# A decoder step on one core: cached latent pages issued from ScalarE's queue, and the first cached sequence's keys and the folding weights loaded during the late prompt attention

## The reference, cut to what matters

```python
def one_seq(args):                       # one of the 8 sequences
    pages, qb, cb, rb = args             # 16 pages of 128 rows, in any order
    c_past = cache_kv_latent[pages].reshape(-1, KV_LORA)      # 2048 x 256
    r_past = cache_k_rope[pages].reshape(-1, QK_ROPE_DIM)     # 2048 x 32
    ...
    k = mla_keys(c_all, r_all, w_uk, g_k_nope, g_k_rope)      # keys, RMS-normalised per head
    p = attn_probs(qb[None], k, mask)
    o_lat = jnp.einsum('bhql,blc->bqhc', p, c_all)            # probabilities times latents
    return jnp.einsum('bqhc,chv->bqhv', o_lat, w_uv)[0]
```

## Time and profile before

| | |
|---|---|
| median of 3 runs | 3511.48 us (3498.91, 3511.48, 3511.61) |
| profiled execution | 3516.18 us, span 3514.4 us |
| TensorE, VectorE, ScalarE, GpSimd busy | 2845.7, 2707.2, 968.1, 1765.9 us |
| DMA | 899.61 MB, mean 256 GB/s over the span |
| sample attention | about 863 to 1265 us of the span |
| late prompt attention | about 615 to 857 us |

### The profile page before, as it was taken

How to read it: one execution, slowest core, us unless ns; L and a number is a source line. 1 busy time by engine, 2 the same in 40 slices (tenths; PEclk the granted TensorE clock), 3 DMA queues, 4 the chain that set the end, 5 groups by cost and what they waited for, 6 DMA issues and landing times. The chain is left out here.

```text
span 3514.4 us, 40173 instructions
## 1 busy us (share of the span) xinstructions
PE 2845.7 (81%) x12509; PEld 2094.9 (60%) x12509; DVE 2707.2 (77%) x5283; ACT 968.1 (28%) x1627; POOL 1765.9 (50%) x1379
## 2 busy tenths in 40 slices
PE   6655697886888866656629799999999999999997
PEld 3444354665333333355618677787778777777775
DVE  3237687896878847759979688888888888888886
ACT  2212132432323311111108622222222222222221
POOL 0026455475545526626546445566666555555553
PEclk9677798876989977787859899999999999999998
DMA  3221587687999968830004689899999988999987
GB/s 117 95 107 48 174 286 275 198 303 265 318 314 337 336 236 325 315 114 31 24 2 192 259 312 332 326 345 335 328 333 340 340 316 333 338 338 338 332 320 263
DMA packets 311112, 899.61 MB, mean 256 GB/s; under 512 B 33641, under 2 KB 125082, under 8 KB 300634
## 3 DMA queue, kind: packets, MB, share of 16 engines
q0 software_dynamic: 156672, 570.49, 45.3%
q1 hardware_dynamic: 152266, 323.70, 25.6%
q10 hardware_dynamic: 2016, 3.67, 0.3%
HBM read 844.35 MB, written 53.64 MB: 256 GB/s over the span
## 5 line engine op out<-in xcount | busy, mean ns | idle before, releaser
L126 POOL DMA_INDIRECT x_got<-v,x_expert x544 | 681.6, 1253 | 649.2 <-DVE x_y L148 501.8
L126 POOL DMA_INDIRECT x_got<-u_rows,x_expert x544 | 723.1, 1329 | 541.3 <-DVE x_got L141 392.8
L148 DVE SCALAR_TENSOR_TENSOR x_y<-x_got,x_hidden,x_y 128x1024 f32<-128x1024 f32 x544 | 695.3, 1301 | 44.2 <-DMA x_got<-v,x_expert 35.0
L141 DVE SCALAR_TENSOR_TENSOR x_got<-x_got,x_y 128x1024 f32<-128x1024 f32 x544 | 647.9, 1221 | 36.0 <-DMA x_got<-u_rows,x_expert 34.3
L1783 PE MATMUL e_a<-h2h,e_uh 128*128 128x512 f32 x1024 | 406.9, 397 | 55.6 <-DVE e_ul L1863 35.9
L1784 PE MATMUL e_a<-h2l,e_uh 128*128 128x512 f32 x1024 | 401.2, 392 | 0.0
L1785 PE MATMUL e_a<-h2h,e_ul 128*128 128x512 f32 x1024 | 401.0, 392 | 0.0
L816 PE MATMUL d_kn<-w_uk_kept,d_page 128*128 128x512 f32 x512 | 256.5, 646 | 52.7 <-DMA d_krT<-page_krT 51.9
L1828 ACT ACTIVATE e_vh<-e_v 128x2048 fp32r<-128x2048 f32 x64 | 122.6, 1916 | 585.1 <-PE e_yt L1802 544.8
L1783 PEld LDWEIGHTS e_a<-h2h,e_uh 128*128 128x128 f32 x1024 | 193.5, 189 | 117.1 <-issue 59.2
L1785 PEld LDWEIGHTS e_a<-h2h,e_ul 128*128 128x128 f32 x1024 | 193.7, 189 | 41.4
(11 more groups left out here) (400 smaller groups left out, 5373.2 us busy)
## 6 DMA issues: line engine op xcount, KB each, us to landing
e_u<-uT SPq DMA_DIRECT2D x128, 512.0 KB, 8.4
e_v<-v SPq DMA_DIRECT2D x64, 1024.0 KB
gates_d<-g_stage SPq DMA_DIRECT2D x8, 4096.0 KB, 11.8
e_gate<-gates_d SPq DMA_DIRECT2D x32, 1024.0 KB
d_page<-page SPq DMA_DIRECT2D x128, 144.0 KB, 4.4
d_latent<-page_rows SPq DMA_DIRECT2D x128, 128.0 KB
x_got<-u_rows,x_expert POOLq DMA_INDIRECT x544, 6.2
x_got<-v,x_expert POOLq DMA_INDIRECT x544, 6.2
```

The costliest lines, as they stand in the source:

```text
L126: pool.indirect_dma_start(out=self.got[row][:], out_offset=None, in_=self.tables[phase], in_offset=bass.IndirectOffsetOnAxis(ap=self.exper ...
L141: dve.scalar_tensor_tensor(out=row[:], in0=row[:], scalar=1.0, in1=self.y[g][:], op0=ALU.mult, op1=ALU.mult, accum_out=self.hidden[:, g, k ...
L148: dve.scalar_tensor_tensor(out=self.y[g][:], in0=row[:], scalar=self.hidden[:, g, k:k + 1], in1=self.y[g][:], op0=ALU.mult, op1=ALU.add).t ...
```

## The change

ScalarE issues the latent pages of a sequence, one after each page's square, with the register read that goes before it, and at page 0 the 4 new rows (`c_now`) as well; SP keeps the keys. The loads of `w_ukT`, `same` and all keys of sequence 0 move into SP's list of the late prompt attention, behind `ident` and `causal`, into space that the input projection's weights `w_in` leave free when the last mixer front has ended; for that, `w_in`'s buffer lives until the sample attention's end. Three semaphores are allocated before the late prompt attention and cleared after the sample attention. Bytes, transfers and arithmetic are the same.

```diff
-def prompt_attention(nc, a, t0, t1, qT, kT, vall, gather, steps):
+def prompt_attention(nc, a, t0, t1, qT, kT, vall, gather, steps, ahead=None):
...
             sp.dma_start(causal[:], a["causal"]).then_inc(s["a_in"], 16)
+            if ahead:
+                ahead(sp)
             for i in range(t0, t1):
...
+FIRST = 4
+
+def first_keys(a, kept, page, krT, w_ukT, same, s):
+    def load(sp):
+        sp.dma_start(w_ukT[:], a["w_ukT"]).then_inc(s["d_ukt"], 16)
+        sp.dma_start(same[:], a["same"]).then_inc(s["d_ukt"], 16)
+        load_keys(sp, a, kept["table"], 0, page, krT, s["d_first0"], s["d_rest0"])
+    return load
+
+def place_of(eng, a, table, b, p):
+    return eng.value_load(table[0:1, bass.ds(b * PAGES + p, 1)], min_val=0, max_val=a["page"].shape[0] - 1)
+
+def load_keys(sp, a, table, b, page, krT, first_in, rest_in):
+    for p in range(PAGES):
+        phys = place_of(sp, a, table, b, p)
+        done = first_in if p < FIRST else rest_in
+        for dst, src in ((page, a["page"]), (krT, a["page_krT"])):
+            sp.dma_start(dst[:, p, :], src[bass.ds(phys, 1)].rearrange("o p c -> (o p) c")).then_inc(done, 16)
...
+        def load_latents(eng, b, e, p):
+            if p == 0:
+                after(eng, s["d_lat"], b - 1)
+                eng.dma_start(c_now[e][:], a["kv_all"][bass.ds(SEQ + b * DEC_S, DEC_S), :]).then_inc(latent_in[e], 16)
+            eng.dma_start(latent_rows[e][:, p, :], a["page_rows"][bass.ds(place_of(eng, a, table, b, p), 1)]
+                          .rearrange("o p c -> (o p) c")).then_inc(latent_in[e], 16)
+
         @block.sync
         def _(sp):
...
-            sp.dma_start(w_ukT[:], a["w_ukT"]).then_inc(s["d_ukt"], 16)
-            sp.dma_start(same[:], a["same"]).then_inc(s["d_ukt"], 16)
-            load_keys(0, 0)
-            load_keys(1, 1)
-            load_latents(0, 0)
-            load_latents(1, 1)
+            load_keys(sp, a, table, 1, page[1], krT[1], first_in[1], rest_in[1])
             for n in range(1, DEC_B - 1):
                 e = (n - 1) % 2
                 sp.wait_ge(s["d_krsq"], n)
                 sp.wait_ge(s["d_sc"], n)
-                load_keys(n + 1, e)
-                sp.wait_ge(s["d_lat"], n)
-                load_latents(n + 1, e)
+                load_keys(sp, a, table, n + 1, page[e], krT[e], first_in[e], rest_in[e])
...
                     act.activation(sq[p % 2][:], kn[p % 2][:, :], ACT.Square,
                                    scale=HD ** -0.5).then_inc(s["d_sq"], 1)
+                    load_latents(act, b, e, p)
...
+            w_in = sb(attention, "w_in_kept", [P, KD, IN_W])
...
+                flat = w_in[:].rearrange("p k c -> p (k c)")
+                at = PAGES * (KVL + ROPE)
+                page0 = flat[:, 0:at].rearrange("p (k c) -> p k c", c=KVL + ROPE)
...
+                begun = {n: nc.alloc_semaphore(n) for n in ("d_ukt", "d_first0", "d_rest0")}
...
+                    prompt_attention(nc, a, TA, PT_TILES, qT, kT, vall, gather, {2: 1, 3: 1, 4: 2, 5: 3, 6: 4, 7: 4},
+                                     first_keys(a, kept, page0, krT0, w_ukT, same, begun))
```

More of the change, by code:

```diff
@@ L59, with with_sems @@
 NEG = -3.0e38
-def with_sems(nc, ctx, names, tag=""):
+def with_sems(nc, ctx, names, tag="", begun={}):
     sems = {n: nc.alloc_semaphore(tag + n) for n in names.split()}
+    sems.update(begun)
     def release():
@@ L676, in _, with sample_attention @@
                     output(n - 1)
-def sample_attention(nc, a, qk_s, kept, gather, steps, gelus):
+FIRST = 4
[13 more added lines that the diff above has]
+            sp.dma_start(dst[:, p, :], src[bass.ds(phys, 1)].rearrange("o p c -> (o p) c")).then_inc(done, 16)
+def sample_attention(nc, a, qk_s, kept, gather, steps, gelus, page0, krT0, w_ukT, same, begun):
     SQ = DEC_S * H
@@ L691, in sample_attention @@
             kept[n] for n in ("ident", "w_uk", "w_uv", "g_k", "newmask", "table"))
-        w_ukT = sb("d_w_ukT", [NOPE, H, KVL])
-        same = sb("d_same", [P, P])
         eps = sb("d_eps", [P, 1])
@@ L697, in sample_attention @@
         qa = sb("d_qa", [P, CT, DEC_B * SQ])
-        page = [sb(f"d_page{e}", [P, PAGES, KVL + ROPE]) for e in range(2)]
+        page = [page0, sb("d_page1", [P, PAGES, KVL + ROPE])]
         latent_rows = [sb(f"d_latent{e}", [P, PAGES, KVL]) for e in range(2)]
-        krT = [sb(f"d_krT{e}", [ROPE, PAGES, P]) for e in range(2)]
+        krT = [krT0, sb("d_krT1", [ROPE, PAGES, P])]
         c_now = [sb(f"d_c_now{e}", [DEC_S, KVL]) for e in range(2)]
@@ L732, in sample_attention @@
         mx_row, mx_col, tot_col = small[0:1, 0:P], small[:, P:P + 1], small[:, 2 * P:2 * P + 1]
-        s = with_sems(nc, ctx, """d_first0 d_first1 d_rest0 d_rest1 d_lt0 d_lt1 d_eps d_qg d_qap d_qa d_mm d_sq d_red d_sc d_raw d_krsq d_krss
+        s = with_sems(nc, ctx, """d_first1 d_rest1 d_lt0 d_lt1 d_eps d_qg d_qap d_qa d_mm d_sq d_red d_sc d_raw d_krsq d_krss
             d_ks1 d_ks2 d_ks3 d_kinv d_new d_smask d_neg d_tr d_nb d_ntr d_nrow d_mx d_mxr d_top d_mxc d_nmx d_exp d_totc d_inv
-            d_ptr d_pt d_ptn d_lat d_ol d_olt d_olT d_op d_o d_ot d_zero d_oT d_st d_ukt""")
+            d_ptr d_pt d_ptn d_lat d_ol d_olt d_olT d_op d_o d_ot d_zero d_oT d_st""", begun=begun)
         first_in = [s["d_first0"], s["d_first1"]]
         rest_in = [s["d_rest0"], s["d_rest1"]]
-        FIRST = 4
         ROTARY = 12
         latent_in = [s["d_lt0"], s["d_lt1"]]
-        n_phys = a["page"].shape[0]
         through = gather.plan(DEC_B * sum(steps))
@@ L2018, in columns @@
                     return out
-                weights = {"w_in": sb(prompt, "w_in_kept", [P, KD, IN_W]), "w_q": sb(prompt, "w_q_kept", [P, QT, H * HD]),
+                weights = {"w_in": w_in, "w_q": sb(prompt, "w_q_kept", [P, QT, H * HD]),
                            "g_kv": sb(prompt, "g_kv_kept", [P, KVL])}
@@ L2027, in build_step @@
                     router(nc, a, 0, TA, [(0, TA * P, (h2h, h2l), [(0, TA * P, 0)])], None, gather, 0, TA)
+                flat = w_in[:].rearrange("p k c -> p (k c)")
+                at = PAGES * (KVL + ROPE)
+                page0 = flat[:, 0:at].rearrange("p (k c) -> p k c", c=KVL + ROPE)
+                w_ukT = flat[0:NOPE, at:at + H * KVL].rearrange("p (h c) -> p h c", c=KVL)
+                at += H * KVL
+                krT0 = flat[0:ROPE, at:at + PAGES * P].rearrange("p (k c) -> p k c", c=P)
+                same = flat[:, at + PAGES * P:at + PAGES * P + P]
+                begun = {n: nc.alloc_semaphore(n) for n in ("d_ukt", "d_first0", "d_rest0")}
                 with nc.sbuf_tensor("qT_late", [P, H, (PT_TILES - TA) * P], F32) as qT:
                     mixer_front(nc, a, TA, TILES, columns(qT, TA), vall, kept, weights, gather, (4, 2, 8))
-                    prompt_attention(nc, a, TA, PT_TILES, qT, kT, vall, gather, {2: 1, 3: 1, 4: 2, 5: 3, 6: 4, 7: 4})
-            sample_attention(nc, a, qk_s, kept, gather, [1, 1, 1, 2] * (PAGES // 4), (0,))
+                    prompt_attention(nc, a, TA, PT_TILES, qT, kT, vall, gather, {2: 1, 3: 1, 4: 2, 5: 3, 6: 4, 7: 4},
+                                     first_keys(a, kept, page0, krT0, w_ukT, same, begun))
+            sample_attention(nc, a, qk_s, kept, gather, [1, 1, 1, 2] * (PAGES // 4), (0,), page0, krT0, w_ukT, same, begun)
         with ExitStack() as peer:
```

## The result

The changed kernel took 3467.1 us (median of 4 runs, 3462.67 to 3479.91) where the kernel before took 3509.8: a ratio of 0.9891, 95% interval 0.9857 to 0.9925. Two later sets on other occasions gave 0.9882 (0.9861 to 0.9903) and 0.9872 (0.9849 to 0.9894). The forecast was 3466 us.

What follows compares the result with a forecast made beforehand. The prediction took SP's full instruction stream in the sample attention as the bound. The start's 16.0 us and the seven periods' 29.3 us sum to 45.3 us, taken from 3511.5 to give 3466 us, range 3446 to 3490.

Steps and rivals of the forecast that it cites:

- What bounds the kernel: Sample attention: SP's instruction stream is full, setting the period of about 45 us; TensorE waits for key pages.
- the rival built on it: Handing issues to another engine saves nothing in the periods; only the start is gained, 3495 us; chance 0.05.
- The start, 16.0 us: Start of the sample attention: early keys and weights save 16.0 us, bounds 4 and 18.
- TensorE's part: At the start, TensorE's first multiplications wait only for VectorE's second scaling: 4.1 us gained.
- The 11.9 us of the stall: First sequence: VectorE's 11.93 us stand, because pages 5 to 16 had not landed, goes.
- The periods, 29.3 us: Seven periods between sequence marks fall from 45.4 to 41.2 us each, saving 29.3 us; bounds 39.5 and 45.0 each.
- The 0.5 us for ScalarE: Added per sequence: an issue before the exponential delays the next square by up to 1.07 us, about half hidden.
- the serial page on ScalarE: Square, then register load with issue, one after the other: 0.60 + 1.07 = 1.67 us a page.
- The late prompt attention, 0: SP's 28 us of extra issues end nine us before its first store wait: cost 0, bounds -1 and +4 us.
- The end of the stage, 0: Tail after the last mark uses the same instructions, last latents needed over 8 us after issue: no change.
- DMA as the bound at 338 GB/s: Rival: a period's 15.2 MB takes 45.0 us, only the start's gain remains, 3495 us; chance 0.10.
- ScalarE as the bound: Rival: dear register loads on ScalarE, break-even 2.0 us a page; at 2.5 us about 3565 us; chance 0.07.

Runs made afterwards that it cites:

- e1: Changed kernel with first sequence's keys, folding weights and `same` loaded at the sample attention's start again, ScalarE keeping the latents; 3483.0 us, 0.9932 of the kernel before.
- e2: Changed kernel with the latents issued by SP again, the early loads staying in the late prompt attention; 3483.6 us, 0.9940 of the kernel before.
- e5: Changed kernel with half of each latent page's bytes loaded, same instruction count; 3453.0 us, 0.9841 of the kernel before.
- e4: Changed kernel with three more register loads on ScalarE before each latent page, values unused; 3513.4 us, 1.0031 of the kernel before.
- e3: Changed kernel with one more register load on ScalarE before each latent page, value unused; 3467.5 us, 0.9891 of the kernel before.

## Why the prediction was right

*What bounds the kernel: right.* SP's instruction stream, read from its even 45 us without a pause, was the bound of the stage: e1 takes 27 us off the stage, and 24 off the median, by moving the latents' issues and nothing else. The Trainium skill (DMA: Bandwidth & Descriptors, Issuing engines are not separate DMA queues) counts the sequencer's time as usually small beside the transfer; here it was the whole period, and the rival built on it fell.

*The start, 16.0 us: measured 15.0* (64.9 to 49.9 us to the first mark). TensorE's part was forecast as 4.1 and was 4.2 (5.0 us after the block's first VectorE instruction before, 0.8 after). The 11.9 us of the stall came back as 10.8; gathered rows, for which VectorE waits 1.6 us before the first mark where it waited 0.8, took most of the rest.

*The periods, 29.3 us: measured 28.0*, at 41.4 us each for 41.2. The unstalled second sequence of the kernel before, 40.7 us, was the right yardstick. The addition to it was right in size and wrong in kind, and that is luck. The 0.5 us for ScalarE did not come: VectorE's waits on squares outside the start are 0.9 us in the whole stage. In its place stand gathered rows, 1.9 us a sequence where the second sequence had 0.9, a growth that the forecast left out. The step that failed is the serial page on ScalarE, 0.60 + 1.07: the load runs beside the square, and square, load and issue together took 1.14 us.

*The late prompt attention, 0: measured +0.6 us*, within its bounds. The cover of nine us at the first store was 9.2.

*The end of the stage, 0: measured 1.6 us longer* (22.2 to 23.8 from the last mark), but the runs with the same code there lie between 21.9 and 24.5, so it is no effect that these runs can tell.

*The sum* of 45.3 us stands against 41.5 in the stage and 41 to 43 between the medians of three sets. That the two terms could be added was not argued in the forecast, and e2 shows that it was only true in the order in which they were taken: the start was priced with SP already relieved. Priced alone, on the kernel before, the early loads are worth 25.0 us of the stage.

*The rivals.* DMA as the bound at 338 GB/s was wrong as a level: the stage runs at 368 from 960 to 1160 us, and with a longer ring at 382. The row was misread in part, too: the stage's slices with 314 to 337 GB/s are the 11th to the 14th, and the best of all 40 is 345; at that rate the rival's period is 44.1 us instead of 45.0. The Trainium skill's limit of about 358 GB/s (DMA: Bandwidth & Descriptors, Specifications) was passed by this mix of gathers and page loads over 200 us. The rival was right as a direction, since e5 shows that bytes still count. ScalarE as the bound is real with three more register loads a page (e4), and not with one (e3).

## What to carry to other kernels

Read an issuing engine's queue for even spacing without a pause: where that spacing equals the period of the stage, the issue is the bound, however idle the engine looks in the busy table, and the price of the fix is found in a stretch of the same trace that happened to run without the wait. Price two edits that relieve the same engine together, not each alone; alone they gave 27 and 25 us of the stage, together 41.5. When an engine and the DMA engines come out as equal bounds and both help by the sum, look at the ring between them first: here one more buffer took away most of the waits that looked like full bandwidth.

## What the runs showed of the hardware that was not expected

A register load in ScalarE's stream runs beside the activation sent off before it: the read started 0.01 us after the square and an issue came 0.70 us after the square's start with one load ahead of it. In e4 a further load cost 0.53 us, and three loads ran under a table load and an exponential.

The DMA share of 1.02 at 368 GB/s in the profile's rows was not full: with six buffers, the same stretch showed 1.05 at 382 GB/s, and one wait of 3.2 us for key pages in the stage.
